# Two fused transformer blocks on one core: separate steps for casts, subtractions, evictions and half units, with the stage borders ordered by hand

## What is computed

```python
# block 1, each of 2 layers
proj = rmsnorm(x) @ w_in                       # 1024 -> 4360 columns
ya = moba_attention(q, k, v) * silu(ag)        # 8 heads, causal, ALiBi
yb = head_norm(retention(...)) * silu(bg)      # 4 heads
yc = head_norm(mlstm(...)) * silu(cg)          # 4 heads
x  = x + concat(ya, yb, yc) @ w_out

# block 2, each of 2 layers; shifts, scales and gates come from silu(c) @ w_ada
x = x + gate1 * swiglu(modulate(norm(x)), w_ffn1)        # 1024 -> 2*2816 -> 1024
x = x + gate2 * merge(neighborhood, window attention, conformer conv)
x = x + gate3 * swiglu(modulate(norm(x)), w_ffn2)
```

## Time and profile before

| | |
|---|---|
| runs | 2641.25 us median (2637.88, 2641.25, 2642.29) |
| profiled execution | 2638.58 us, its span 2636.8 us |
| PE busy | 2457.2 us, 93% of the span, 13210 matmuls |
| DVE busy | 1600.4 us, 61% |
| ACT busy | 877.7 us, 33% |
| POOL busy | 222.6 us, 8% |
| chain that ended last | PE 77%, DVE 13%, ACT 5%, issue 3% |
| mean granted TensorE clock | 0.945 of full |

### The profile page before, as it was taken

One profiled execution on the slowest core, in us unless ns is written; L12 is line 12 of the kernel. 1 busy time (PEld: TensorE's weight loads), 2 busy tenths in 40 slices (PEclk: granted clock), 3 DMA queues, 4 the chain that ended last, 5 costly groups with the idle time before them and its releaser, 6 DMA issues.

```text
span 2636.8 us, 33057 instructions
## 1 busy us (share of the span) xinstructions
PE 2457.2 (93%) x13210; PEld 2077.3 (79%) x13210; DVE 1600.4 (61%) x2950; ACT 877.7 (33%) x1488; POOL 222.6 (8%) x321
## 2 busy tenths in 40 slices
PE   5888887799999999989989999989999999998998
PEld 5777776688888876668888888888888887788998
DVE  3875875577767445554458986654443345665665
ACT  3343433322222333333332222232222234344443
POOL 1000000100001200001111111100000020011000
PEclk9898987799999897999989999989999989798999
DMA  6533542254444310112325655522322232134553
GB/s 227 180 121 104 175 136 72 75 173 168 168 167 152 96 62 22 37 54 86 101 80 192 237 210 203 191 85 88 100 93 95 96 104 84 52 121 152 183 184 122
DMA packets 95353, 332.99 MB, mean 126 GB/s; under 512 B 11040, under 2 KB 13216, under 8 KB 94816
## 3 DMA queue, kind: packets, MB, share of 16 engines
q1 hardware_dynamic: 70496, 244.41, 27.2%
q0 software_dynamic: 23376, 84.80, 10.0%
q10 hardware_dynamic: 1328, 1.66, 0.2%
HBM read 329.78 MB, written 2.48 MB: 126 GB/s over the span
## 4 chain that ended last, share of the span: by engine, by line
PE 77%; DVE 13%; ACT 5%; issue 3%; POOL 1%; DMA 1%; ACTq 0%; POOLq 0%; DVEq 0%
PE PS L417 76%; DVE WL L1083 3%; ACT WH L794 2%; DVE ST L1096 1%; DVE NT L1092 1%; PE PS L720 1%; ACT P L795 1%; DVE AR L1093 1%; DVE JK L1093 1%; DVE HL L1092 1%; DVE PJ L1092 1%; DVE CV L1092 1%; ACT PT L794 1%; POOL SS L1672 1%; DMA CST<-in_cst 0%
## 5 line engine op out<-in xcount | busy, mean ns | idle before, releaser
L417 PE MATMUL PS<-HH,WH 128*128 128x512 f32 (+1 forms) x2136 | 772.3, 362 | 21.7 <-DVE HL L1092 21.4
L1083 DVE TENSOR_TENSOR WL<-RAW,WH 128x1024 fp32r<-128x1024 f32 (+2 forms) x482 | 575.4, 1194 | 324.7 <-ACT WH L794 323.6
L417 PE MATMUL PS<-HL,WH 128*128 128x512 f32 (+1 forms) x2136 | 758.9, 355 | 0.0
L417 PE MATMUL PS<-HH,WL 128*128 128x512 f32 (+1 forms) x2136 | 758.8, 355 | 0.0
L794 ACT ACTIVATE WH<-RAW 128x1024 fp32r<-128x1024 f32 (+2 forms) x482 | 490.4, 1019 | 247.5 <-PE PS L417 247.5
L417 PEld LDWEIGHTS PS<-HH,WH 128*128 128x128 f32 x2136 | 415.1, 194 | 95.1 <-DVE HL L1092 28.6
L417 PEld LDWEIGHTS PS<-HL,WH 128*128 128x128 f32 x2136 | 416.0, 195 | 56.4
L417 PEld LDWEIGHTS PS<-HH,WL 128*128 128x128 f32 x2136 | 415.2, 194 | 56.8
L417 PE MATMUL PS<-GH,WH 128*128 128x512 f32 (+1 forms) x776 | 270.8, 349 | 0.0
L417 PE MATMUL PS<-GH,WL 128*128 128x512 f32 (+1 forms) x776 | 270.7, 349 | 0.0
L417 PE MATMUL PS<-GL,WH 128*128 128x512 f32 (+1 forms) x776 | 270.5, 349 | 0.0
(11 more groups left out here) (219 smaller groups left out, 3125.1 us busy)
## 6 DMA issues: line engine op xcount, KB each, us to landing
RAW<-in_wst SPq DMA_DIRECT2D x420, 512.0 KB, 3.5
AR<-in_w_adaT POOLq DMA_DIRECT2D x144, 512.0 KB, 3.7
RAW<-in_wst SPq DMA_DIRECT2D x48, 384.0 KB, 3.0
BM<-rpb_rows POOLq DMA_DIRECT2D x48, 64.0 KB, 2.6
CB<-in_cc POOLq DMA_DIRECT2D x2, 1024.0 KB, 9.9
RAW<-in_wst SPq DMA_DIRECT2D x8, 256.0 KB, 2.7
RAW<-in_wst SPq DMA_DIRECT2D x4, 396.0 KB, 5.3
rpb_rows<-in_rpb POOLq DMA_DIRECT2D x2, 697.5 KB, 10.0
```

The costliest lines, as they stand in the source:

```text
L417: return e.matmul(o, l, r, start=start, stop=stop)
L1083: return e.tensor_tensor(out=o, in0=a, in1=b, op=op)
```

## The change

It splits what one D did into separate letters. D is now half of a dense step on TensorE (12 of the 24 matmuls), so every D count doubles and `mix` spreads the others among halves. Three new letters carry the rest: H is one cast on ScalarE, S one subtraction on VectorE, V the evictions of one dense step on all engines. A pass at the end of `plan()` places them: after the first half of a step H for the unit that is due, after the second half S for it and V; with `lag = 0` (block 1) V is the eviction of this step, with `lag = 1` (block 2) that of the step before, and there it comes right behind H, in the middle of the next step. The letter F evicts all that is outstanding, and so does the start of a norm outside the borders. The borders are spelt letter by letter in `BORDER`. In block 1 the last two M parts before the output product also move behind an F.

```diff
 def mix(**steps):
     out = []
     for name, n in steps.items():
+        if name == "D":
+            n *= 2
         out += [((2 * i + 1) / (2 * n), name) for i in range(n)]
...
-    def boundary(last):
-        if last:
-            return ["D", "N", "D", "N", "N", "N", "N", "D"] + ["N"] * 5 + ["D"]
-        return ["N", "N", "D"] + mix(D=1, N=8) + ["D"] * HELD
+    BORDER = ["("]
+    BORDER += ["D", "V", "N", "D", "N", "V"]
+    BORDER += ["D", "H", "N", "N", "D", "S", "N", "V"]
+    BORDER += ["D", "H", "N", "N", "D", "N", "V"]
+    BORDER += ["D", "N", "N", "S", "N", "H", "D", "N"]
+    BORDER += ["D", "N", "N", "S", "D", "V", "N", "N"]
+    BORDER += ["D", "N", "V", "D", "N", "N"]
+    BORDER += ["D", "V", "N", "D"] + [")"] + ["D"] * 4
...
-        order += mix(D=2, A=3, M=4)
+        order += mix(D=2, A=3, M=2) + ["F", "M", "M"]
...
-        out += mix(B=nb - b0, P=4, C=9)
+        out += ["F"] + mix(B=nb - b0, P=4, C=9)
...
-    B = ["D"] * HELD
-    order += B + NORM + B
+    B = ["D", "D"] * HELD
+    order += ["1"] + B + NORM + B
...
+        elif name in "01":
+            lag = int(name)
+        elif name == "F":
+            until("V", n["D"] // 2)
...
+            if name == "D" and not by_hand:
+                e = n["D"] // 2
+                if n["D"] % 2:
+                    until("H", due[e + 1])
+                    until("V", e)
+                else:
+                    until("S", due[e])
+                    until("V", e - lag)
...
         def dense():
             for x in S:
                 u, un = x.u, U[x.u]
+                todo = [(j, k) for j in range(len(x.tiles)) for k in range(un.kt)]
...
+                for y, (j, k) in enumerate(todo):
+                    d = x.tiles[j]
+                    if y == len(todo) // 2:
+                        yield
...
-        def dense():
-            silu = [0]
-            for u in range(NS):
-                high(u)
+        def casts():
+            for u in range(NU):
+                high(u)
+                if u >= NS - 1:
+                    yield
+
+        def evictions():
+            silu = [0]
             for e_ in S:
```

More of the change, by code:

```diff
@@ L100, in plan @@
     for l in range(DEPTH):
-        order += NORM
+        order += ["0"] + NORM
         feat("w_in", l, 3072, 4, "cp", "H1", l, 256)
@@ L212, in plan, with until @@
             S[e + 1].split.append(u + NS)
+    due = [1]
+    for x in S:
+        due.append(due[-1] + len(x.split))
+    out, n, by_hand, lag, norm = [], dict(D=0, V=0, H=0, S=0), False, 0, 0
+    def until(name, k):
+        out.extend([name] * max(0, k - n[name]))
+        n[name] = max(n[name], k)
+    for name in order:
+        if name in "()":
+            by_hand = name == "("
+        elif name in "01":
[3 more added lines that the diff above has]
+        else:
+            if name == "N":
+                if norm % 10 == 0 and not by_hand:
+                    until("V", n["D"] // 2)
+                norm += 1
+            out.append(name)
+            if name in n:
+                n[name] += 1
+            if name == "D" and not by_hand:
[3 more added lines that the diff above has]
+                    until("V", e)
+                else:
+                    until("S", due[e])
+                    until("V", e - lag)
+    order = out + ["V"] * (len(S) - n["V"])
     return U, S, T, order, ropes
@@ L474, in dense @@
                     P = PS[T[d].bank]
[L475 to L488, removed]
+                    a, z = un.first and k == 0, un.last and k == un.kt - 1
+                    c = slice(128 * j, 128 * j + 128)
+                    if un.mode == "f":
+                        xh, xl = operand(un, k, T[d].halves)
+                        m = T[d].cols
+                        mm(P[:, 0:x.n], wh[:, k, c], xh[:, m], a, False)
+                        mm(P[:, 0:x.n], wh[:, k, c], xl[:, m], False, False)
+                        i = mm(P[:, 0:x.n], wl[:, k, c], xh[:, m], False, z)
+                    else:
+                        xh, xl = operand(un, k, range(x.n // 2))
+                        mm(P[:, 0:un.cols], xh[:, c], wh[:, k, :], a, False)
+                        mm(P[:, 0:un.cols], xl[:, c], wh[:, k, :], False, False)
+                        i = mm(P[:, 0:un.cols], xh[:, c], wl[:, k, :], False, z)
+                    if k < un.kt - 1:
+                        continue
                     if x.closes and d == x.tiles[-1]:
@@ L1075, in scalar_program @@
         q.wait_ge(d_cst, 32)
-        return dict(D=dense(), N=norm(), M=mlstm(), T=retention(), A=attention1(), B=attention2(), L=lnorm(), E=ada())
+        return dict(H=casts(), N=norm(), M=mlstm(), T=retention(), A=attention1(), B=attention2(), L=lnorm(), E=ada(), V=evictions())
     def vector_program(e):
@@ L1107, in low, with splits, evictions @@
                 *vd.inc("wl", u))
-        def dense():
+        def splits():
+            for u in range(NU):
+                low(u)
+                if u >= NS - 1:
+                    yield
+        def evictions():
             silu = [0]
-            for u in range(NS):
-                low(u)
             for e_ in S:
                 un = U[e_.u]
-                for u in e_.split:
-                    low(u)
                 for d in e_.tiles if un.last else ():
@@ L1783, in misc @@
                 yield
-        return dict(D=dense(), N=norm(), M=mlstm(), T=retention(), L=lnorm(), E=ada(), K=misc())
+        return dict(V=evictions(), N=norm(), M=mlstm(), T=retention(), L=lnorm(), E=ada(), K=misc())
     def sync_program(e):
```

19 lines of the change are left out of this document (8 added, 11 removed).

## The result

The changed kernel takes 2555.98 us (median of four runs, 2551.03 to 2561.51) against 2640.68 us for the kernel before (2637.88 to 2642.29) on the same chip. The ratio is 0.9681, 95% interval 0.9656 to 0.9705. That is 85 us faster, where 37.5 us were forecast.

What follows compares the result with a forecast made beforehand. TensorE, busy 93% of the span, was taken as the bound, with only idle time and lower-clock time to win. Terms -26 - 15 + 3 - 9 + 9.5 = -37.5 us gave 2603 us; 8-in-10 range 2582 to 2636.

Steps and rivals of the forecast that it cites:

- the borders: Four borders: earlier tokens' broadcast and no 4.10 us wait for ScalarE give 6.5 us each, -26 us.
- the later evictions: Value projections: lagged evictions make TensorE wait 1.75 us for QA and 2.2 us for V; +9.5 us in all.
- the FFNs: FFNs: later evictions still leave 9 us to spare before a bank is needed; 0.
- (a): Borders: the chain forms again on VectorE, 2 us per border, 2621 us; chance 0.18, alone or with (d).
- (c): Borders: short waits keep TensorE at 1.2 GHz throughout, +9 us each, 2665 us; chance 0.10 for this or worse.
- (d): Block 1: VectorE's order makes subtractions late, 2626 us alone, 2644 with (a); chance 0.06 for both together.
- term 2: Block 1's attention: half units between A letters win 10 us of idle time and 5 of lost clock; -15 us.
- the first mixer's gates: First mixer: B letters spread among half units cover 12 short waits; -9 us, ends 0 and 15.7.
- the second mixer: Second mixer: units of 256 columns and few paired B, so 0.
- Term 3: Block 1's front: M parts go ahead of subtractions, costing +1.5 us a layer, +3 us in all.
- The case of many short waits: Borders: four short waits in place of two would spend clock rather than win it; priced as (c).
- (b): Borders, attention and mixer: everything fits better, borders give 10 us each, attention and mixer 8 more, 2581 us; chance 0.13.

Runs made afterwards that it cites:

- run 5: Changed kernel with the two halves of each dense step side by side in block 1 only; 2586.50 us, ratio 0.9804.
- run 2: Changed kernel with the four old borders put back, everything else as changed; 2591.35 us, ratio 0.9802.
- run 7: Changed kernel with two flushes of due evictions, before and right behind each value projection; 2547.42 us, ratio 0.9653.
- run 9: Run 7's kernel with the mixer's eight steps spread over all but eight attention parts, rope and convolution thinner; 2542.83 us, ratio 0.9652.
- run 10: Run 7's kernel with each mixer's first two gate steps moved into the stretch where attention ran alone; 2537.65 us, ratio 0.9624.
- run 11: Run 5's kernel with six useless matmuls ahead of each block 1 attention product after the second; 2591.45 us, ratio 0.9834.
- run 6: Changed kernel with the two last M parts back among block 1's attention parts; 2558.94 us, ratio 0.9697.
- run 1: Kernel before with only the four new borders; 2607.38 us, ratio 0.9869.
- run 3: Changed kernel with whole dense steps everywhere outside the borders; 2608.64 us, ratio 0.9877.

## Why the prediction was wrong

**The direction and most of the mechanisms held.** What was priced from rows of waits came out: -28.2 against -26 for the borders, +10.1 against +9.5 for the later evictions, with both waits right to 0.06 us, and 0 in the FFNs. Rivals (a) and (c) did not happen: no long wait on WL or SM, and the borders' clock rose from 0.81 to 0.85 to 0.91 to 1.00. Of (d) next to nothing is there: the stretch between the front and the attention takes 58.3 us in layer 0 (58.9 before) and 59.9 in layer 1 (58.7 before).

**The step that failed is term 2**, block 1's attention, forecast at -15 and measured at -29.5 in the profiles and at 32 us by run 5 for the half steps in all of block 1. "Of 21.7 us idle in the two stretches I count 10 as won" was near: in stretches about as long as those of the forecast (155.0 to 205.9 and 367.6 to 424.5 before) idle time fell by 11.9 us, in the longer ones of the table by 7.5 and 8.3. "A third of it goes, -5" was the mis-sized part. At the same work busy time fell by 2.1 and 11.6 us, 13.7 in all. In the part of layer 1 from 353.9 to 394.0 us the changed kernel has no half-clocked time at all, where the 63 us of the earlier trace rows ran at 0.78; runs 2, 7, 9 and 10, with the same block 1, have 6.8 us there, still far under the 22.7 of before. I took the lost clock as a cost of its own that would mostly stay. It was for the most part the consequence of the waits: run 11 fills waits with useless work and the clock comes back. It does not return wait by wait: in layer 0's first part idle time fell from 10.6 to 3.8 us and the half-clocked time stayed (6.6 and 6.8 us).

Two readings inside the step were wrong as well. The waits for O were said not to depend on the half steps: 2.38 and 2.49 us became 0.68 and 1.00. Run 6, with the M parts as before, has 2.38 and 1.00, so the moved M parts shorten the first one and the rest of the change the second. Run 5, with whole steps, keeps 2.97 us for PT: it is the waits for PT that the half steps take away. And no wait above 1.6 us was to be left: there are three, 1.89 and (in layer 1) 1.88 for TM and 1.75 for O. The two for TM come with the moved M parts and are gone in run 6.

**The same step failed elsewhere.** In the first mixer's gates all 4.5 us of lost clock went, not a part, -13.4 against -9. For the second mixer I wrote "few paired B: 0"; it is 5.5 us shorter although it now carries the V wait, at a clock of 0.95 against 0.89 (2 to 4 us shorter in runs 5, 6 and 11). For the borders I credited nothing to the clock, because four short waits seemed to remain; the first border has two. The total fitted, 28.2 for 26, but its parts did not: only 24.4 - 12.1 = 12.3 us are idle time, where the 6.5 us a border were reckoned from shorter waits alone. The other 16 are busy time, hence clock. That the sum came out there is in part luck. Summed over the kernel I had put some 7 us on the clock and taken 3 off for the value projections; it gave 48.

**Term 3 had the wrong sign.** The front of block 1 was forecast at +1.5 a layer. Up to the same cast (96.1 and 308.9 us before) it is 2.9 and 1.8 us shorter. The gates' matmul waits 2.42 us instead of 4.63:

```profile
63.84 0.55 PE L458 MATMUL PS<-H1H,WH 128*128 128x256 f32 x1 [3.65 <-DVE WL L1131]
70.38 0.76 PE L458 MATMUL PS<-WH,H1H 128*128 128x512 f32 x1 [2.19 <-DVE WL L1131]
78.64 0.39 PE L458 MATMUL PS<-MA,CST 128*128 128x8 f32 x2 [2.42 <-DVE MA L1140]
```

TensorE now waits longer at 63.84 (2.11 us before), as reckoned, but shorter for the gates. Why the half unit that I counted as still to do costs nothing behind them is not shown. With whole steps (run 5) the cast comes 3.0 us later again. The size is unsure: in runs 2, 7, 9 and 10, with the same front, layer 0 comes to this cast only 0.4 to 0.9 us earlier than before, though nowhere later.

**The case of many short waits did not arise.** I had expected four short waits in a border in place of two, and the clock hung on that. Over the whole kernel TensorE has fewer waits: counted from the traces, 42 waits above 1 us against 57 before, and 41 between 0.3 and 1 us against 38. Half-clocked time fell from 294 to 170 us. The Trainium skill (TensorE: Matmul & The Clock Gate, section "A second HAM failure mode: psum-queue depth-cycling") would have frequent short pauses make the clock swing; since they did not become more frequent, no run here tests it. I had given that side 0.10; what stood on the other side, rival (b) with 0.13 and a price of only -22, was too small because it too counted the clock as a fraction.

## What to carry to other kernels

Where TensorE is the bound and its clock is below full, price every wait twice, by its own length and by the half-clocked matmuls behind it. Where a change takes most waits of a stretch away, give the sum a range up to the whole of the lost clock: here all of it went in the first mixer's gates, 48 of 58 us of half clock in the four borders, and none in the first part of layer 0's attention. Halving long dense steps and spreading small dependent work between them takes waits away with no new instruction. Evictions behind a cast cost where the next matmul takes the same bank at once: flush there.

## What the runs showed that I had not expected

- Useless matmuls nearly pay for themselves: 42 us of them cost 6 us in the two stretches and 8 in the whole kernel (run 11).
- The same border order shows different clocks: 1.00 in borders 1 and 4 of the changed kernel, 0.91 in its border 3 with nearly the same two first waits (0.79 us on SQ, then 1.83 or 1.84 on DG). Its first border has no half-clocked time in the changed kernel and in six of the runs, and 6.8 us in runs 1, 3, 6, 10 and 11. The Trainium skill (TensorE: Matmul & The Clock Gate, section "Part 1: The HAM clock gate (the "warmup" mystery)") says that the monitor runs on its own time, whatever the kernel does, so that one kernel can meet it differently from run to run; these rows agree. Such differences set a floor of a few us to what one profile can tell of a stretch.
- The lag and its removal take the same time (0.9681 and 0.9688) with 10 us moved from one place to the other. A change that measures as nothing can be a gain and a cost: runs 7 and 10 keep the lag and drop its cost at the value projections.
